# Order of the wide and narrow matmul runs in an eight-slab group: twos against fours

## What is computed

```python
def conv_ffn(h, w_up, conv_w, conv_b, w_down):
    S = h.shape[1]
    u = h @ w_up
    up = jnp.pad(u, ((0, 0), (CONV_WIDTH - 1, 0), (0, 0)))
    u = conv_b + conv_w[0] * up[:, 0:S] + conv_w[1] * up[:, 1:S + 1] + conv_w[2] * up[:, 2:S + 2]
    g, val = u[..., :D_FF], u[..., D_FF:]
    return (jax.nn.silu(g) * val).astype(h.dtype) @ w_down

for layer in range(DEPTH):                                 # DEPTH = 2
    h = rmsnorm(x, g_mix_pre[layer])
    y = (even_mixer if layer % 2 == 0 else odd_mixer)(h, ...)   # h @ w_in: q, k, v
    x = x + rmsnorm(y, g_mix_post[layer])
    h = rmsnorm(x, g_mem_pre[layer])
    y = memory_cross_attention(h, memn, ...)
    x = x + rmsnorm(y, g_mem_post[layer])
    h = rmsnorm(x, g_ffn_pre[layer])
    y = conv_ffn(h, w_up[layer], conv_w[layer], conv_b[layer], w_down[layer])
    x = x + rmsnorm(y, g_ffn_post[layer])
```

## Time and profile before

| | |
|---|---|
| median of three runs | 2431.17 us (2430.42 to 2433.34) |
| the profiled execution | 2429.3 us |
| its span on the core | 2427.5 us |
| PE busy | 2413.0 us, 99% of the span |
| DVE busy | 1861.2 us, 77% |
| ACT busy | 1384.1 us, 57% |
| slab transfers (q1) | 447.83 MB, 58.7% of 16 DMA engines' span |

### The profile page before, as it was taken

One profiled execution on the slowest core, in us unless ns is written; L12 is line 12 of the kernel. 1 busy time (PEld: TensorE's weight loads), 2 busy tenths in 40 slices (PEclk: granted clock), 3 DMA queues, 4 the chain that ended last, 5 costly groups with the idle time before them and its releaser, 6 DMA issues.

```text
span 2427.5 us, 35035 instructions
## 1 busy us (share of the span) xinstructions
PE 2413.0 (99%) x12548; PEld 2068.5 (85%) x12548; DVE 1861.2 (77%) x2559; ACT 1384.1 (57%) x1960; POOL 55.7 (2%) x108
## 2 busy tenths in 40 slices
PE   9999999999999999999999999999999999999998
PEld 7888888888888888888888888888888888888887
DVE  7768877678777777888876588776787777778887
ACT  6545665665555555555555456666655555555554
POOL 0000000000000000000000003000000000000000
PEclk9999999999999999999999999999999999999999
DMA  8766556466565565766766675564665656567665
GB/s 303 239 203 217 159 161 191 146 215 193 188 191 191 185 195 183 226 206 211 230 184 192 189 221 185 163 188 155 209 198 182 196 181 195 183 192 229 202 213 186
DMA packets 252095, 477.85 MB, mean 197 GB/s; under 512 B 18257, under 2 KB 21473, under 8 KB 251969
## 3 DMA queue, kind: packets, MB, share of 16 engines
q1 hardware_dynamic: 234640, 447.83, 58.7%
q10 hardware_dynamic: 17328, 28.35, 3.7%
HBM read 468.89 MB, written 6.31 MB: 196 GB/s over the span
## 4 chain that ended last, share of the span: by engine, by line
PE 94%; DVE 2%; DMA 1%; ACT 1%; issue 1%; POOL 0%; ACTq 0%; POOLq 0%; DVEq 0%; SPq 0%
PE acc L2384 16%; PE acc L2392 8%; PE tp L2384 8%; PE aux L2384 8%; PE acc L2336 7%; PE acc L2337 7%; PE acc L2335 7%; PE acc L2329 5%; PE acc L2331 5%; PE acc L2330 5%; PE aux L2392 4%; PE tp L2392 4%; PE acc L2356 1%; PE aux L2356 1%; PE tp L2335 1%; DVE w_lo L1371 1%
## 5 line engine op out<-in xcount | busy, mean ns | idle before, releaser
L1371 DVE TENSOR_TENSOR w_lo<-raw,w_hi 128x1024 fp32r<-128x1024 f32 x847 | 1015.9, 1222 | 354.3 <-ACT w_hi L651 351.3
L651 ACT ACTIVATE w_hi<-raw 128x1024 fp32r<-128x1024 f32 x847 | 882.7, 1055 | 579.8 <-PE aux L2384 105.0
L2384 PE MATMUL acc<-a_hl,w_hi 128*128 128x512 f32 x1664 | 514.5, 390 | 0.9 <-DVE rope_sin L1585 0.9
L2384 PEld LDWEIGHTS acc<-a_hl,w_hi 128*128 128x128 f32 x1664 | 305.6, 188 | 58.8 <-issue 1.5
L2392 PE MATMUL acc<-a_hl,w_lo 128*128 128x256 f32 x1664 | 334.5, 283 | 0.0
L2392 PEld LDWEIGHTS acc<-a_hl,w_lo 128*128 128x128 f32 x1664 | 266.2, 191 | 8.1
L2384 PE MATMUL tp<-a_hl,w_hi 128*128 128x512 f32 x832 | 256.6, 389 | 0.0
L2384 PE MATMUL aux<-a_hl,w_hi 128*128 128x512 f32 x832 | 256.5, 389 | 0.0
L2329 PE MATMUL acc<-w_hi,a_hl 128*128 128x512 f32 x476 | 191.1, 401 | 1.9 <-DVE a_hl L1400 1.1
L2331 PE MATMUL acc<-w_hi,a_hl 128*128 128x512 f32 x476 | 186.1, 391 | 0.0
L2330 PE MATMUL acc<-w_lo,a_hl 128*128 128x512 f32 x476 | 185.5, 390 | 0.0
(11 more groups left out here) (390 smaller groups left out, 3478.1 us busy)
## 6 DMA issues: line engine op xcount, KB each, us to landing
raw<-in_w_up SPq DMA_DIRECT2D x352, 512.0 KB, 4.6
raw<-in_w_down SPq DMA_DIRECT2D x176, 512.0 KB, 4.9
raw<-in_w_in_c SPq DMA_DIRECT2D x96, 512.0 KB, 4.3
raw<-in_w_in_ab SPq DMA_DIRECT2D x95, 512.0 KB, 4.7
raw<-in_w_out_ab SPq DMA_DIRECT2D x32, 512.0 KB, 3.7
raw<-in_w_out_c SPq DMA_DIRECT2D x32, 512.0 KB, 3.7
raw<-in_w_mk SPq DMA_DIRECT2D x16, 512.0 KB, 4.9
raw<-in_w_mq SPq DMA_DIRECT2D x16, 512.0 KB, 4.2
```

The source lines that it names most:

```text
L651: act.activation(w_hi[:, s % RING], raw[:, s], ACT.Copy).then_inc(hi_ready, 1)
L1371: dve.tensor_tensor(w_lo[:, s], raw[:, s], w_hi[:, s % RING].bitcast(F32), ALU.subtract).then_inc(lo_ready, 1)
L2384: last = pe.matmul(bank, w_hi[:, (slot + i) % RING, j, f * P:(f + 1) * P], both, start=(kt == 0), stop=(kt == KT - 1))
```

## The change

The runs are four slabs long. A group's order becomes: wide 0 to 3, narrow 0 to 3, narrow 4 to 7, wide 4 to 7. SP's wait for the raw slots follows: slots 0 to 3 of a group are now free when the wide half of slab 4 is done, whichever of the four it is, and slots 4 to 7 each after its own wide half.

```diff
+RUN = 4
...
-                    sp.wait_ge(slab_used, n - (RAW - 1) + (2 if in_twos(n, up) else 0))
+                    sp.wait_ge(slab_used, n - (RAW - 1) + (RUN - s if in_runs(n, up) and s < RUN else 0))
...
-                    if in_twos(n + RING, True):
+                    if in_runs(n + RING, True):
                         act.wait_ge(lo_ready, n - (RING - 1))
...
-            def two_slabs_turned(n, slot, par, k0):
+            def run_turned(n, slot, par, k0):
...
-                wide_first = (k0 // SLAB_KT) % 4 == 0
+                wide_first = k0 == 0
                 for part in (0, 1):
-                    for i in range(2):
+                    for i in range(RUN):
...
-                        elif s % 2 == 0:
-                            two_slabs_turned(n + s, s % RAW, par, SLAB_KT * s)
+                        elif s % RUN == 0:
+                            run_turned(n + s, s % RAW, par, SLAB_KT * s)
...
-                        elif q % 2 == 0:
-                            two_slabs_turned(n + q, q % RAW, q // GS, SLAB_KT * (q % GS))
+                        elif q % RUN == 0:
+                            run_turned(n + q, q % RAW, q // GS, SLAB_KT * (q % GS))
```

More of the change, by code:

```diff
@@ L424, in gain, with in_runs @@
             return gT[:, PRE[sub[0]], sub[1], kt:kt + 1]
-        def in_twos(n, up):
+        def in_runs(n, up):
             if not isinstance(n, int):
```

## The result

The changed kernel takes **2632.35 us** (median of five runs, 2629.27 to 2640.74). The kernel before took 2432.22 us beside it (five runs, 2430.42 to 2434.14). The ratio is 1.0826, 95% interval 1.0815 to 1.0838: 8.3% slower. The number lies in the predicted range, 69 us above the forecast and within 4 us of rival (b).

What follows compares the result with a forecast made beforehand. PE's matmul row bounds the kernel, busy 2413.0 of 2427.5 us. Terms 116 + 8 + 10 − 1.6 = 132 us on the profiled 2429.3 give 2561.7; with 1.9 for the median, 2563 us, 5.4% slower, range 2505 to 2640.

Steps and rivals of the forecast that it cites:

- rival (b): Up groups: clock halves after each wait, 1.9 us a fall, +73 us in 38 groups, 2636 us; chance 0.15.
- The price of the row: PE's matmul row: one wide/narrow switch fewer per group, 0.03 us each in 52 groups, 1.6 us gained.
- The mechanism and its size: Up groups: late reload delays slab 6's low part, PE waits 3.05 us in each of 38 groups, 116 us.
- Slab 14 of the early pairs: First two up pairs per layer: next-stage blocks on ACT and DVE delay slab 14 by 2 us, 8 us in four groups.
- The clock stays at 1.00: Up groups: PE keeps its full clock despite the waits, so no added matmul price; part of the 2563 us forecast, chance 0.57.
- The 10 us for query/key: Query and key: slower transfers beside other traffic cost 2.5 us at two group changes per layer, 10 us (0 to 25).
- The floor of 2.0 us: Up groups: the new order alone, nothing else moved, makes slabs 6 and 7 late by 2.0 us per group.
- rival (a): Up groups: order alone costs 2.0 us in each of 38, transfers in time; about 2510 us, chance 0.13.
- Rival (d): Up groups: slab 6's low part in time, its chain 1.8 us shorter; 2429.5 us, chance 0.05 together with an ineffective change.
- The transfers: Slab loads in a burst: issued 0.45 us apart, first landing after 3.9 us, the others 1.35 us apart.

Runs made afterwards that it cites:

- e3: Changed kernel with convolution taps behind the splits of slabs 6 and 7, and slots 0 to 3 reloaded after their own narrow halves: 2431.52 us, ratio 0.9999.
- e2: Changed kernel with slots 0 to 3 each reloaded as soon as their own narrow half is done: 2458.49 us, ratio 1.0111.
- e1: Changed kernel with ACT's and DVE's convolution taps moved behind the splits of slabs 6 and 7: 2465.71 us, ratio 1.0143.
- e7: Changed kernel, but slots 0 to 3 all released together when narrow half 7 is done: 2499.69 us, ratio 1.0269.
- e4: Changed kernel plus ten unused matmuls ahead of slab 6's narrow half in each of 40 up groups: 2595.88 us, ratio 1.0672.
- e6: Changed kernel, but slots 0 to 3 all released together when narrow half 3 is done: 2457.87 us, ratio 1.0103.

## Why the prediction was right, and where it fell short

**The price of the row.** Forecast 1.6 us gained for 52 groups. Right in sign: e3 shows 0.4 us per up stage, 0.8 for 40 groups where 1.2 was forecast, two thirds of the size.

**The mechanism and its size.** Shown right. The reload of slots 0 to 3 is late (first issue at T − 5.1, as forecast), slab 3's split holds ACT's copies (T + 3.98, forecast 3.85), slab 6's low part is ready at T + 16.0 (860.76, forecast 15.9), and PE waits 2.86 us (forecast 2.9). In the 38 groups that were forecast to pay, the waits before slab 6 are 113.9 us against 116. The first group of each layer was counted at nothing, as still under the old wait. It paid 1.2 and 0.9 us: SP's loop sets the new wait for its slabs too (e2). e1 removes one half of the cause and e2 the other, and each takes nearly all of the idle time away (111.6 us before narrow halves, 2.1 in e1, 9.3 in e2).

**Slab 14 of the early pairs.** Forecast 8 us for four groups. They last 28.0, 27.9, 28.9 and 29.1 us against 26.8 for the others: 7 us. Only 3 of them are wait, which is 3.7 us in these groups and 2.9 in the others; the 2 us of work delay slab 14 by 0.8, not by 2.

**"The clock stays at 1.00".** This is the step that failed. It was written into the likeliest case with the argument that 2.9 us "may end just short of it"; rival (b) had it right, at 15%. Its price was well sized: 1.9 us a fall forecast, 1.7 measured (57.0 / 33). That its 2636 us stands so near the measured 2632 is in part luck: it counts 38 falls where up had 32, and nothing for the 13.6 us of the next paragraph. The evidence lay in the earlier trace rows: the clock fell some 2.5 us after the last matmul, the forecast wait was longer, and I still gave the one instance less weight than the hope that 2.9 would escape. Two measurements back the price: 57.0 us by the distances between starts, and at least 36 us by e4, which does more work and is faster. The Trainium skill (TensorE: Matmul & The Clock Gate, "What's actually happening") calls the throttled clock the default that activity lifts; the trace agrees, with 34 falls, each around a wait of PE, though eight of the waits in up passed without one.

**The stages between and behind the runs.** Not in the sum at all: 13.6 us, shown by e1 to be the reload's own cost, since it stays when the waits in up are gone and leaves with e2. Half of it stands right behind the runs (the four waits, 6.2 us). Most of the rest stands just ahead of up, near 494 and 1813 us, where PE now waits for a low part of the stage's activations (section 5 of the page, before and changed):

```profile
L2329 PE MATMUL acc<-w_hi,a_hl 128*128 128x512 f32 x476 | 191.1, 401 | 1.9 <-DVE a_hl L1400 1.1
...
L2330 PE MATMUL acc<-w_hi,a_hl 128*128 128x512 f32 x476 | 191.8, 403 | 6.6 <-DVE a_hl L1410 5.0
```

The 1.1 us of the kernel before are one wait at its start; the 5.0 of the changed kernel are two, and they make the matmuls behind them 3.0 and 3.3 us later, the second with a fall of the clock. There SP issues the first eight slabs of up in one burst, because its loop sets the late wait for them too, ACT waits 4.3 and 4.1 us for the first, and the activations stand behind it on ACT and DVE. The 10 us for query/key were right in kind and measured 13.5. The same omission made the expectations of e1 and e4 some 20 us too low, though the trace of the change already had the number.

**The floor of 2.0 us.** Wrong, and it didn't show in the forecast because another term covered it. With the transfers in time the order alone costs 0.63 us a group (e2), so rival (a) at 2510 us was 50 too high. I took slab 5's start on DVE, T + 6.4, as given by DVE's own work, and said that "nothing gives way". But the row shows ACT waiting 1.88 us for slab 5's transfer. The change releases slots 4 to 7 earlier: the prediction itself put slot 5's issue at T − 2.9. Rival (d) named this link and asked for 1.8 us; e2 gave about 1.5, which is why slab 6 is still a little late there.

**The transfers.** Slabs 0 to 3 landed 1.33 to 1.8 us apart, against 1.35, and the first 3.7 after its issue; the issues are 0.56 us apart (839.6 to 842.4 for six), against 0.45, which cost nothing, since the transfers behind each other are slower than that. The Trainium skill (DMA: Bandwidth & Descriptors, "Anatomy of one DMA — SWDGE (gpsimd) path") gives its fit for transfers that GpSimd issues, which the prediction did not say; these are issued by SyncE. The estimates by that fit, 3.2 and 1.2 us, are below the measured 3.7 and 1.33 to 1.8, and the forecast would have been further off with them.

By the medians the miss is 69 us. The profiled execution, whose rows give the terms, lies higher: its 211.5 us are 79 above the 132 of the sum. The clock is 57 of them, the stages between and behind the runs 13.6, query/key 3.5, and the rest is small.

**Two causes that are worth 30 us each are worth 200 together.** All four kernels have the runs of four on PE. Late reload with the taps out of the way: 33 us (e1). Taps in the way and an early reload: 26 us (e2). Neither: nothing that the medians can tell (e3). Both: 200 us. In the kernel before, slab 6's low part had 1.9 us to spare. The order takes that and 0.63 more; the reload alone delays a chain that e1 has taken out of the way. Only together does every microsecond of delay of slab 3 become a microsecond of PE's, as e7 and the changed kernel show, and only then are the waits long enough for the clock.

What stays open: why eight of the 40 waits in up passed without a fall of the clock, six of them 2.4 to 2.8 us long, and what all of the 14.3 us spread over the other distances are. A part may be slab 7's narrow half: in e2, where the clock does not fall, its distances are 6.7 us over the usual in 38 groups, 0.18 each, and the prediction gave slab 7 0.2. No run here separates the rest.

## What to carry to other kernels

When a change takes a buffer's release later, follow the late transfer through every in-order engine to the work queued behind it: here it was a PSUM copy on ACT and the taps on DVE that made PE wait, hardly ever the slab itself. Before a step's own time is taken as fixed, look at what ended the idle time ahead of it. If it was a transfer that the change moves, the step moves too. And where a forecast puts a wait of some microseconds on TensorE into every group, price the clock with it, from whichever row of the trace shows it fall.

## What the runs showed of the hardware

- The clock fell to 1.2 GHz around 32 of the 40 waits before slab 6 in up, which were 2.9 us long on average (the longest 3.7), and around two other waits; twice with 38 waits of 1.3 us (e7, the longest 2.9), and never in e2, where they were 1.0 us at most. The length of the wait alone does not decide: in e7 it fell around a wait of 2.2 us and stayed up through one of 2.4. I had not expected it to follow waits of that length so regularly.
- In the group shown, the half clock lies not in the wait but in the work after it: PE starts again at 860.76, the clock falls at 861.3, and PE is busy for all of 862 to 864 at 0.50, with the matmuls at nearly twice their price.
- Unused matmuls in the wait pay for themselves: ten per group made the kernel 36 us faster, five per group 29. It is no remedy for the wait, only for its second price.
- Six 512 KB transfers issued within 2.8 us landed 3.7 to 8.0 us after their issues, one every 1.33 to 1.8 us: in a burst the landings set the pace, not the issues. Issued early enough (e6), a burst costs nothing.
